# Starting the moving operand's slices at different offsets modulo 512 bytes in a two-block fp32r transformer kernel on one core

## What is computed

```python
def first_block(x, p, ...):                     # x: 512 x 1024
    h = rms_norm(x, norm1_g)
    proj = h @ w_in                             # 1024 x 3080
    mixed = concat(gated_deltanet, multiscale_pool, short_gated_conv)
    x = x + mixed @ w_out
    h = rms_norm(x, norm2_g)
    x = x + (silu(h @ w_gate) * (h @ w_up)) @ w_down      # width 2816
    x = x + sigmoid(x @ ple_gate) * (p @ ple_proj)
    return rms_norm(x, final_g)

def second_block(x, ...):
    mix = token_mixer(rmsnorm(x))               # mLSTM heads and latent attention, w_in 1024 x 1960
    x = x + rmsnorm(mix)
    y = square(relu(rmsnorm(x) @ w_up)) @ w_down          # width 4096
    return x + rmsnorm(y)
```

## Time and profile before

| | |
|---|---|
| runs | 1485.9, 1487.42, 1488.25 us |
| median | 1487.42 us |
| profiled execution, first to last instruction | 1483.7 us |
| TensorE busy in it | 1378.8 us (93%) |
| VectorE, ScalarE, GpSimd busy | 624.3, 522.2, 524.7 us |
| mean granted TensorE clock | 0.970 of full speed |

### The profile page before, as it was taken

The page is one execution under the profiler, slowest core; times in us unless marked ns, Lnnn a source line. Parts: engine busy times, 40 slices in busy tenths (PEclk is TensorE's granted clock), DMA queues, the critical chain, the costliest instruction groups (busy, mean ns, idle before and its releaser), DMA issues.

```text
span 1483.7 us, 15766 instructions
## 1 busy us (share of the span) xinstructions
PE 1378.8 (93%) x6297; PEld 1087.8 (73%) x6297; DVE 624.3 (42%) x847; ACT 522.2 (35%) x795; POOL 524.7 (35%) x230
## 2 busy tenths in 40 slices
PE   4899989999999999999988987978979999999997
PEld 3677888867888888888865855544748888888885
DVE  6557866156211121121366934355156532414223
ACT  4477112355222222221445423455244322313232
POOL 2233241133544544543532322210313444444441
PEclk7899999999999999999998999999989999999998
DMA  5222210122333333332332231100112333333321
GB/s 163 57 72 57 58 29 15 57 85 74 110 91 95 99 100 92 93 99 78 107 85 64 58 71 43 43 29 1 57 57 71 99 100 91 96 98 99 91 80 57
DMA packets 215456, 112.19 MB, mean 76 GB/s; under 512 B 15116, under 2 KB 213592, under 8 KB 215384
## 3 DMA queue, kind: packets, MB, share of 16 engines
q1 hardware_dynamic: 214584, 110.34, 26.1%
q10 hardware_dynamic: 672, 0.79, 0.2%
q0 software_dynamic: 128, 0.07, 0.0%
HBM read 109.08 MB, written 2.10 MB: 75 GB/s over the span
## 4 chain that ended last, share of the span: by engine, by line
PE 84%; DVE 11%; ACT 3%; issue 2%; DMA 0%; POOL 0%; DVEq 0%; ACTq 0%; SPq 0%
PE bank L1654 22%; PE bank L1656 22%; PE bank L1655 22%; PE aux L1829 2%; PE aux L1011 1%; PE aux L1842 1%; PE bank L1677 1%; PE bank L1679 1%; PE bank L1678 1%; PE aux L1839 1%; PE bank L996 1%; PE aux L937 1%; PE aux L925 1%; PE aux L939 1%; DVE rstd L2197 1%
## 5 line engine op out<-in xcount | busy, mean ns | idle before, releaser
L1616 POOL TENSOR_TENSOR wl<-raw,wh 128x1024 fp32r<-128x1024 f32 (+1 forms) x203 | 502.4, 2477 | 899.1 <-ACT wh L1933 898.7
L1654 PE MATMUL bank<-ah,wh 128*128 128x512 f32 x1024 | 407.7, 398 | 0.1
L1656 PE MATMUL bank<-al,wh 128*128 128x512 f32 x1024 | 400.0, 391 | 0.0
L1655 PE MATMUL bank<-ah,wl 128*128 128x512 f32 x1024 | 400.0, 391 | 0.0
L1933 ACT CAST wh<-raw 128x1024 fp32r<-128x1024 f32 (+1 forms) x203 | 210.4, 1039 | 393.1 <-PE bank L1656 380.5
L1654 PEld LDWEIGHTS bank<-ah,wh 128*128 128x128 f32 x1024 | 193.2, 189 | 45.9 <-issue 6.0
L1655 PEld LDWEIGHTS bank<-ah,wl 128*128 128x128 f32 x1024 | 193.2, 189 | 40.4 <-issue 1.4
L1656 PEld LDWEIGHTS bank<-al,wh 128*128 128x128 f32 x1024 | 192.9, 188 | 40.6
L1654 PE MATMUL bank<-yh,wh 128*128 128x512 f32 x432 | 171.2, 396 | 0.0
L1656 PE MATMUL bank<-yl,wh 128*128 128x512 f32 x432 | 170.6, 395 | 0.0
L1655 PE MATMUL bank<-yh,wl 128*128 128x512 f32 x432 | 170.6, 395 | 0.0
(11 more groups left out here) (377 smaller groups left out, 1593.4 us busy)
## 6 DMA issues: line engine op xcount, KB each, us to landing
raw<-in_w_up SPq DMA_DIRECT2D x54, 512.0 KB, 4.0
raw<-in_w_down SPq DMA_DIRECT2D x48, 512.0 KB, 4.1
raw<-in_w_in SPq DMA_DIRECT2D x41, 512.0 KB, 3.9
raw<-in_w_gate SPq DMA_DIRECT2D x22, 512.0 KB, 3.8
raw<-in_w_out SPq DMA_DIRECT2D x16, 512.0 KB, 4.0
raw<-in_ple_gate SPq DMA_DIRECT2D x8, 512.0 KB, 3.8
raw<-in_w_down SPq DMA_DIRECT2D x8, 384.0 KB, 3.3
xtok<-in_x SPq DMA_DIRECT2D x4, 512.0 KB, 5.2
```

What stands on the lines that cost most here:

```text
L1616: nc.gpsimd.tensor_tensor(wl[b % SPLIT][:, 0:w], raw[b % RAW][:, 0:w], wh[b % SPLIT][:, 0:w].bitcast(F32), ALU.subtract).then_inc(wl_ready, 1)
L1654: nc.tensor.matmul(ps, h[:, c:c + P], mh[:, k, :], start=(n == 0), stop=False)
L1655: nc.tensor.matmul(ps, l[:, c:c + P], mh[:, k, :], start=False, stop=False)
L1656: last = nc.tensor.matmul(ps, h[:, c:c + P], ml[:, k, :], start=False, stop=(n == nk - 1))
```

## The change

The eight slices of `ah` become eight tensors that start at 0, 32, 64 ... 224 bytes past their old places, and those of `al` at 256, 288 ... 480 bytes past theirs. The four hidden tiles start at 384, 448, 640 and 768 bytes past their old places. Since those were at offset 128, the new offsets modulo 512 are 0 for `yh[0]`, 64 for `yh[1]`, 256 for `yl[0]` and 384 for `yl[1]`; inside one of these tiles all slices keep one offset. The pads behind them are 512 and 1024 bytes, so every other tile keeps its offset modulo 512, the weights among them. No instruction is added, removed or moved.

```diff
+AH_SKEW = tuple(range(0, 256, 32))
+AL_SKEW = tuple(range(256, 512, 32))
+SKEW_PAD = 512
+Y_SKEW = (384, 448, 640, 768)
...
+def of_k(mov, k):
+
+    return mov[k][:, :] if isinstance(mov, list) else mov[:, k, :]
...
-        ah = sb("ah", [P, KD, T], F32R)
-        al = sb("al", [P, KD, T], F32R)
+        at = top[0]
+        ah = [sb(f"ah{k}", [P, T], F32R, at=at + k * 4 * T + AH_SKEW[k]) for k in range(KD)]
+        at += KD * 4 * T
+        al = [sb(f"al{k}", [P, T], F32R, at=at + k * 4 * T + AL_SKEW[k]) for k in range(KD)]
+        top[0] = at + KD * 4 * T + SKEW_PAD
...
-        yh = [sb(f"yh{i}", [P, KD, T], F32R) for i in range(2)]
-        yl = [sb(f"yl{i}", [P, KD, T], F32R) for i in range(2)]
+        hids = [sb(f"y{'hl'[i // 2]}{i % 2}", [P, KD, T], F32R, at=free + i * KD * 4 * T + Y_SKEW[i]) for i in range(4)]
+        yh, yl = hids[0:2], hids[2:4]
+        top[0] = free + 4 * KD * 4 * T + 1024
...
-                    nc.tensor.matmul(ps, h[:, c:c + P], mh[:, k, :], start=(n == 0), stop=False)
-                    nc.tensor.matmul(ps, l[:, c:c + P], mh[:, k, :], start=False, stop=False)
-                    last = nc.tensor.matmul(ps, h[:, c:c + P], ml[:, k, :], start=False, stop=(n == nk - 1))
+                    nc.tensor.matmul(ps, h[:, c:c + P], of_k(mh, k), start=(n == 0), stop=False)
+                    nc.tensor.matmul(ps, l[:, c:c + P], of_k(mh, k), start=False, stop=False)
+                    last = nc.tensor.matmul(ps, h[:, c:c + P], of_k(ml, k), start=False, stop=(n == nk - 1))
```

More of the change, by code:

```diff
@@ L873, in by_token @@
                         h, l = wh[b % SPLIT][:, o:o + width], wl[b % SPLIT][:, o:o + width]
-                        nc.tensor.matmul(ps, mh[:, k, s], h, start=(k == 0), stop=False)
-                        nc.tensor.matmul(ps, mh[:, k, s], l, start=False, stop=False)
-                        last = nc.tensor.matmul(ps, ml[:, k, s], h, start=False, stop=(k == nk - 1))
+                        nc.tensor.matmul(ps, of_k(mh, k)[:, s], h, start=(k == 0), stop=False)
+                        nc.tensor.matmul(ps, of_k(mh, k)[:, s], l, start=False, stop=False)
+                        last = nc.tensor.matmul(ps, of_k(ml, k)[:, s], h, start=False, stop=(k == nk - 1))
                     last.then_inc(gemm_done, 1)
@@ L1676, in gemm_pair @@
                         ps = bank[u % NBANK][:, :]
-                        nc.tensor.matmul(ps, wh[b][:, c], ah[:, k, :], start=(n == 0), stop=False)
-                        nc.tensor.matmul(ps, wl[b][:, c], ah[:, k, :], start=False, stop=False)
-                        last = nc.tensor.matmul(ps, wh[b][:, c], al[:, k, :], start=False, stop=(n == KD - 1))
+                        nc.tensor.matmul(ps, wh[b][:, c], ah[k][:, :], start=(n == 0), stop=False)
+                        nc.tensor.matmul(ps, wl[b][:, c], ah[k][:, :], start=False, stop=False)
+                        last = nc.tensor.matmul(ps, wh[b][:, c], al[k][:, :], start=False, stop=(n == KD - 1))
                         if n == KD - 1:
@@ L1978, in upper @@
                 act.wait_ge(*wait)
-                nc.scalar.copy(ah[:, k, :], src).then_inc(ah_ready, 1)
+                nc.scalar.copy(ah[k][:, :], src).then_inc(ah_ready, 1)
             tables(LN_EXP_TABLES)
@@ L2188, in lower @@
                 dve.wait_ge(ah_ready, KD * fill + i + 1)
-                nc.vector.tensor_tensor(al[:, k, :], src, ah[:, k, :].bitcast(F32), ALU.subtract).then_inc(al_ready, 1)
+                nc.vector.tensor_tensor(al[k][:, :], src, ah[k][:, :].bitcast(F32), ALU.subtract).then_inc(al_ready, 1)
             def add_square(n, k):
```

## The result

| | before | after |
|---|---|---|
| median, us | 1487.48 (1485.9 to 1488.25, 4 runs) | 1498.76 (1498.54 to 1499.6, 4 runs) |
| span of the profiled execution, us | 1483.7 | 1497.1 |
| mean granted TensorE clock | 0.970 | 0.967 |

A forecast was written before the change was run, and what follows sets the result against it. Time was taken as the number of fp32r matmuls times the distance between their starts. 16.6 - 1.0 + 0.3 = +15.9 us on the 1483.7 span gives 1499.6, plus 3.7 to the median: 1503 us, range 1472 to 1522.

The forecast's parts named there:

- Its last step: Whole kernel: the median of the runs lies 3.7 us above the profiled span, taking 1499.6 to 1503 us.
- The `ah` and `al` streams: fp32r matmuls with ah and al moving: 2860 lose the even rhythm and cost 5.8 ns more each, +16.6 us.
- "Settled" streams: fp32r matmuls: operands all sharing one offset can settle into an even 226.7 ns; unsettled streams cost about 232 to 233 ns.
- The hidden tiles: 1296 matmuls with yh and yl moving: unsettled again, 232.5 ns in place of 233.3, -1.0 us.
- `ah` and `al` as stationary operands: 192 matmuls of 256 columns with ah and al stationary: 0 to 1.3 us, taken as +0.3 us.
- Writing and other reading: ScalarE and VectorE writing ah and al, and output stores: 0, with bounds of 1 us and 0.3.
- B: Moving operands at odd multiples of 32: 237.5 ns or more throughout, much slower, 1527 us; chance 0.10.
- C: Every fp32r matmul: weight load collides with the moving stream, most new offsets part them, 20.6 us less, 1467 us; chance 0.26.
- D: fp32r rate comes from something the change keeps, or the rhythm survives small steps: no change, 1487 us; chance 0.16.

The follow-up runs named there:

- `half_0_32`: Kernel after, with slices 0 to 3 of ah and al at 0 and 4 to 7 at 32 (modulo 256), hidden tiles at 0; 1499.99 us.
- `y_only`: Kernel after, with ah and al back at offset 0 and the hidden tiles left as changed; 1484.87 us.
- `ah_only`: Kernel after, with the hidden tiles back at offset 128 and ah and al left as changed; 1500.78 us.
- `all_zero`: Kernel after, with ah, al and all four hidden tiles at offset 0, the offset of the weights; 1480.25 us.
- the map: Four variants of the kernel after with fixed offsets for ah, al and the hidden tiles, one run each; 1488.2, 1499.86, 1504.53 and 1489.5 us.
- `weights_128`: Moving operands as in the kernel before, only the weights wh and wl 128 bytes further on; 1497.56 us.
- `map_96_192_480`: Kernel after, with ah and al fixed at 96, yh[0] and yl[0] at 192, yh[1] and yl[1] at 480; 1504.53 us.
- `steps_64`: Kernel after, with ah and al going up by 64 bytes per slice in place of 32, hidden tiles at 0; 1493.35 us.

## Why the prediction was right, and where not

**The forecast and the range** held: slower, 1498.8 in 1472 to 1522, though 11.3 us slower and not 15.6. The forecast was made as +15.9 us on the profiled span; the span grew by 13.4. Its last step, 3.7 us from span to median, was too large: a run's time lies only 1.8 us above its own span (1498.92 and 1497.1 after), so the span of 1483.7 was that of a short execution, and half of the 3.7 was spread between runs.

**The `ah` and `al` streams**, forecast at 232.5 ns and +16.6 us, came to 232.5 ns and +17.0. This is no luck of two errors. Of the 3183 distances under 250 ns before, 2872 were 226 or 227 ns, where the prediction took 2860 as settled, and these lost the 5.8 ns; the other 311, at 231.7 ns on average, lost about 0.8. The reason given was half right. "Settled" streams and the cost of leaving that state are real, as the `half_0_32` tile shows. But variation is not needed: a fixed offset of 32, 96 or 160 costs as much with none at all. How the 5.8 ns divide between the offsets themselves and their changes is not known, since the rates of the single slices follow neither theory. That two different reasons lead to the same 232.5 ns, because nearly every offset costs about 233, is luck.

**The hidden tiles** are the step that failed. It was put as "they are unsettled again, 232.5", -1.0 us; they gave -5.6 us, which is most of what the forecast missed. The words for it were that a stream settles when its operands all share one offset; `yh[0]` and `yl[0]` are 256 apart and settled fully. The unit is 256 bytes, not 512, and nothing in the trace before could show that, since it had only the offsets 0, 128 and 192. The prediction named the test that would part it (chunks 0 and 2 against 1 and 3), and it came out as 227 against 231 ns.

**`ah` and `al` as stationary operands**, forecast at +0.3 us: the distances between such matmuls that follow each other at once at full clock went down, from 119.8 to 118.2 ns on average, but the 190 distances add up to 24.2 us in place of 23.0, because of the stretch at the 1.2 GHz level shown above. That the change moved the stretch there is not shown; `y_only` and `ah_only` have it too, `all_zero` has not. A small term with an unexpected sign in its rate, see below.

**Writing and other reading**, forecast at 0: ScalarE's copies to `ah` have a median of 620 ns (619 before), VectorE's to `al` 684 (684), and the output stores land in 2.8 us (2.7).

**The rivals.** B had its 237.5 ns in no stretch as a mean; the highest was 234.3, at 160. C is excluded by the map at every offset tried. D's reason, that the place in memory and not the relation matters, is excluded by `weights_128`.

What stays open is the resource. The runs show that the rate depends on the address of the moving stream relative to the weights, modulo 256, and that a change is felt for some six matmuls; that the weights' load is what meets the stream is likely, but argued. At equal addresses a matmul costs 13.3 ns above the 213.3 of its columns, at most others 20. Whether the 13.3 ns at offset 0 would be there without a weight load was not tried.

One more thing in the traces narrows it: at the 1.2 GHz level the offset costs nothing. Three distances between matmuls with `ah` at 0, in the kernel before, and three at 96, in `map_96_192_480`, with the stretch's row (length, TensorE busy, clock) ahead of each:

```profile
790.00:791.50 1.50, 1.50 (x5) 0.50 0.00 0
790.66 0.63 PE L1678 MATMUL bank<-ah,wl 128*128 128x512 f32 x1
...
791.94 0.63 PE L1678 MATMUL bank<-ah,wl 128*128 128x512 f32 x1
```

```profile
803.00:805.50 2.50, 2.50 (x7) 0.50 0.00 0
803.40 0.63 PE L1692 MATMUL bank<-al,wh 128*128 128x512 f32 x1
...
804.68 0.63 PE L1692 MATMUL bank<-al,wh 128*128 128x512 f32 x1
```

Both take 1.28 us, 427 ns a matmul, and every trace has 36 to 49 such distances of 426 or 427 ns whatever its offsets. 427 ns is twice 213.3, so at this level only the columns are left, and the 13.3 to 20 ns appear at 2.4 GHz alone.

The totals are softer than the rates. `half_0_32` and `steps_64`, equal in the stretch, differ by 6.6 us in a single run each; their three fp32r streams differ by 0.8 us in all, the rest lies between other matmuls. Part of the TensorE stages run at the 1.2 GHz level, for 88 to 112 us of the span in the various traces, 112 in `half_0_32` and 98 in `steps_64`; how much of that difference comes from it was not separated.

## What to carry to other kernels

Where fp32r matmuls of 512 columns stream back to back, each with its own weight load, look at the distance from start to start at the 2.4 GHz level and put the moving operand at the same offset modulo 256 bytes as the weights; here that was worth 6.6 ns of 233 for each, and the one-line pad of `all_zero` brought 0.5%. Spreading buffers over many offsets to avoid conflicts did the opposite. Test such a thing by moving the other operand as well: if the rates change places, it is the relation that counts.

## What had not been expected of the hardware

- At the 1.2 GHz level the offset makes no difference: 426 or 427 ns for 512 columns at offset 0, at 96 and with mixed offsets.
- The period of 256 bytes, with a dip at 64 (228.9 ns, as at 320) between 233.3 ns at 32 and at 96.
- With `ah` stationary and 256 columns of weights moving, offset 0 is not the cheap one: 119.8 ns between starts before, 118.2 in the kernel after and 118.0 in `map_96_192_480`. The middle line of `by_token` before, and then after:

```profile
L875 PE MATMUL bank<-wl,ah x64: 278/283/283, 815.8 to 845.4; 128*128 128x256 f32 x64
```

```profile
L888 PE MATMUL bank<-wl,ah x64: 276/280/420, 823.9 to 854.5; 128*128 128x256 f32 x64
```

- Several offsets settle into fixed cycles of unequal distances with the same mean: at 128, 229 and 238 ns in turn; at 96, 231, 231 and 238; in chunk 1 of the kernel after, 233, 236 and 224.
